# States summed on GpSimd, swapped stationaries, one transpose per four heads, and a rotary swap by DMA

## The reference, cut to what matters

```python
z = rmsnorm(h) @ w_in                       # q, kc, vc, ksl, vsl, kw, vw, gates, u
q, kc, ksl, kw = rope(...)                  # [x1*cos - x2*sin, x1*sin + x2*cos] by half heads of 32
kcmp = gelu((blocks(kc) + pe_k) @ wk1) @ wk2   # blocks of 32 tokens, stride 16: 31 of them, 2 groups
vcmp = gelu((blocks(vc) + pe_v) @ wv1) @ wv2
o = g0*softmax(q kcmp) vcmp + g1*softmax(q ksl) vsl + g2*softmax(q kw) vw
# S5: complex state per channel, x[t] = a*x[t-1] + bu[t];  y = Re(C x) + d*u;  gelu, GLU
h = h + concat(o, o_s5) @ w_out
```

## Time and profile before

| | us |
|---|---|
| median of 3 runs | 2008.1 (2006.92 to 2008.7) |
| the profiled execution: its time | 2005.77 |
| its span | 2004.0 |
| PE busy in the span | 1936.8 (97%) |
| POOL busy in the span | 336.2 (17%) |
| mean granted clock of TensorE | 0.985 |

### The profile page before, as it was taken

The page is one execution under the profiler, slowest core; times in us unless marked ns, Lnnn a source line. Parts: engine busy times, 40 slices in busy tenths (PEclk is TensorE's granted clock), DMA queues, the critical chain, the costliest instruction groups (busy, mean ns, idle before and its releaser), DMA issues.

```text
span 2004.0 us, 22537 instructions
## 1 busy us (share of the span) xinstructions
PE 1936.8 (97%) x9022; PEld 1509.8 (75%) x9022; DVE 1185.7 (59%) x1519; ACT 820.9 (41%) x1210; POOL 336.2 (17%) x329
## 2 busy tenths in 40 slices
PE   7999999999998999999999899999999899999997
PEld 5788888777644788888888778776788778776786
DVE  5748344576764556656655787826753659446732
ACT  5332233311555343213333448545542466445531
POOL 2000000135320110101011212504201024115002
PEclk9999999999998999999999899999999899999998
DMA  5232223222002145645632222221223222221331
GB/s 196 93 106 94 93 96 116 78 74 97 27 1 69 55 151 195 221 141 185 215 111 80 77 93 85 87 95 40 74 95 95 85 82 84 89 80 32 95 98 60
DMA packets 53464, 197.27 MB, mean 98 GB/s; under 512 B 6000, under 2 KB 6512, under 8 KB 52848
## 3 DMA queue, kind: packets, MB, share of 16 engines
q1 hardware_dynamic: 43200, 160.55, 24.4%
q0 software_dynamic: 7648, 29.10, 4.6%
q10 hardware_dynamic: 2512, 6.18, 0.9%
HBM read 192.67 MB, written 2.10 MB: 97 GB/s over the span
## 4 chain that ended last, share of the span: by engine, by line
PE 78%; DVE 13%; ACT 4%; issue 2%; POOL 2%; DMA 1%; ACTq 0%; POOLq 0%; DVEq 0%
PE PS L593 77%; DVE AR L1644 3%; DVE WLO L1641 2%; DVE AR L2170 1%; ACT WHI L1179 1%; DVE AR L1674 1%; DVE TMP L2244 1%; DVE AR L1995 1%; PE PS L843 1%; DVE AR L2137 0%; DMA H<-in_xT 0%; POOL ACC L2302 0%; DVE H L2073 0%; POOL AR L2339 0%; ACT SQ L1194 0%
## 5 line engine op out<-in xcount | busy, mean ns | idle before, releaser
L593 PE MATMUL PS<-HNH,WHI 128*128 128x512 f32 x1632 | 659.3, 404 | 16.4 <-ACT HNH L1210 14.6
L1641 DVE TENSOR_TENSOR WLO<-RAW,WHI 128x1024 fp32r<-128x1024 f32 (+1 forms) x272 | 374.9, 1381 | 506.7 <-ACT WHI L1179 506.6
L593 PE MATMUL PS<-HNH,WLO 128*128 128x512 f32 x1632 | 641.8, 393 | 5.9 <-DVE WLO L1641 5.9
L1179 ACT ACTIVATE WHI<-RAW 128x1024 fp32r<-128x1024 f32 (+1 forms) x272 | 297.7, 1095 | 642.2 <-PE PS L593 583.1
L593 PE MATMUL PS<-HNL,WHI 128*128 128x512 f32 x1632 | 436.3, 391 | 0.1
L593 PEld LDWEIGHTS PS<-HNH,WHI 128*128 128x128 f32 x1632 | 309.1, 189 | 96.3 <-issue 22.1
L593 PEld LDWEIGHTS PS<-HNH,WLO 128*128 128x128 f32 x1632 | 309.5, 190 | 80.4 <-issue 9.1
L593 PEld LDWEIGHTS PS<-HNL,WHI 128*128 128x128 f32 x1632 | 307.6, 188 | 64.8 <-DVE HNL L1644 1.0
L2302 POOL TENSOR_TENSOR ACC<-ACC,SQ 128x512 f32<-128x512 f32 x46 | 62.4, 1356 | 809.8 <-ACT SQ L1194 808.8
L593 PE MATMUL PS<-AR 32*128 32x256 f32 (+14 forms) x844 | 162.3, 414 | 4.4 <-POOL AR L2339 1.7
L593 PE MATMUL PS<-HIDH,WLO 128*128 128x512 f32 x352 | 137.1, 390 | 0.0
(11 more groups left out here) (314 smaller groups left out, 2295.4 us busy)
## 6 DMA issues: line engine op xcount, KB each, us to landing
RAW<-in_w_in SPq DMA_DIRECT2D x80, 512.0 KB, 3.5
AR<-in_w_ada POOLq DMA_DIRECT2D x48, 512.0 KB, 4.1
RAW<-in_w13a SPq DMA_DIRECT2D x44, 512.0 KB, 3.4
RAW<-in_w13b SPq DMA_DIRECT2D x44, 512.0 KB, 3.6
RAW<-in_w_out SPq DMA_DIRECT2D x40, 512.0 KB, 3.5
RAW<-in_w2a SPq DMA_DIRECT2D x16, 704.0 KB, 4.0
RAW<-in_w2b SPq DMA_DIRECT2D x16, 704.0 KB, 5.1
RAW<-in_w_inA SPq DMA_DIRECT2D x12, 512.0 KB, 3.4
```

What stands on the lines that cost most here:

```text
L593: return pe.matmul(o, l, r, start=start, stop=stop, skip_group_check=True)
L1179: act.activation(hi_of(name, i), raw_of(name, i), ACT.Copy).then_inc(*HI.up(name, i))
L1641: dve.tensor_tensor(lo_of(name, i), raw_of(name, i), f32(hi_of(name, i)), S_).then_inc(*LO.up(name, i))
```

## The change

Four edits, all in the mixer.

1. **States summed on GpSimd.** After `back_v` of the second tile, POOL adds the products in `SQ` into `V_`, in two operations of 128 x 512 elements. `read` then needs eight matmuls of the 16, and waits for these two sums.
2. **Compression's positions stationary.** `squeeze` moves the weights (128 columns) past the positions (62 columns stationary), with the two halves of the hidden layer on different output partitions of one bank. The hidden layer comes out turned over, so a step `hidden` transposes it back by two transposes, with two copies on ACT. The step `compressed 1` moves one item later, and writes the compressed values to four groups of partitions (eight small matmuls instead of four, four copies instead of one).
3. **Four heads per transpose.** Four transposes of 128 columns of `CE` serve two head pairs, at i = 0 and i = 2, with one copy on ACT each.
4. **The swap by DMA.** A step `swap` on ACT's queue issues four DMAs of 32 partitions each, from `TMP` to a buffer `TURNED` in SBUF; DVE's `turn` waits for them. PE has no turn any more.

Two `TURNED` buffers lie where `VT` comes later, so ACT's eviction of `v` waits for turn 7. `out_s5` passes over bank 7 where it would be next.

```diff
@@ mix_order @@
+        if i and i != 2:
+            yield "swap", i - 1          # after qk/rope i, before turn
...
+            if (z, tt) == (0, 0):
+                yield "swap", 7
...
+            if (z, tt) == (0, 1):
+                yield "hidden", 0
...
         if n == 4:
+            yield "hidden", 1
+        if n == 5:
             yield "compressed", 1
@@ pe_program @@
-                    for z in range(4):
+                    for z, (name, wr, wl) in enumerate((("state_re", CpR, CaR), ("state_im", CpI, CaI))):
+                        pe.wait_ge(*G.at(name, b))
                         for now in (True, False):
                             for j in range(2):
...
-                elif step == "turn":
-                    ps, b = take(pe, "turn", i)
-                    pe.wait_ge(*V.at("rope", i))
-                    mm(ps[:, :], ROT, TMP[:, i % 4, :], True, True).then_inc(*P_.up("turn", i))
...
-                            t = mm(hc_banks[z][mt][0][:, 0:62], w[:, i, P * mt:P * mt + P],
-                                   XBp[:, ii, :, :].rearrange("p g c -> p (g c)"), ii == 0, ii == 15)
+                            t = mm(hc_banks[z][0][64 * mt:64 * mt + 62, 0:P], XBp[:, ii, :, :].rearrange("p g c -> p (g c)"),
+                                   w[:, i, P * mt:P * mt + P], ii == 0, ii == 15)
...
+                elif step == "hidden":
+                    for mt in range(2):
+                        pe.wait_ge(*A.at("hidt", z, mt))
+                        pe.transpose(ps[:, 0:62], HIDt[r, :], IDENT[r, r]).then_inc(*P_.up("hidden", z, mt))
...
-                    if part == 0 and kind == 2:
-                        for hf in range(2):
-                                t = pe.transpose(ps[0:31, P * qt:P * qt + P], CE[:, qt, 2 * i + hf, 0:31], IDENT)
+                    if part == 0 and kind == 2 and i % 2 == 0:
+                            t = pe.transpose(ps[:, P * qt:P * qt + P], CET[i // 2][:, qt, :], IDENT)
@@ act_program @@
+                elif step == "swap":
+                    act.wait_ge(*V.at("rope", i))
+                    if n > 1:
+                        act.wait_ge(*V.at("turn", TURNS[n - 2]))
+                    for r in range(4):
+                        act.dma_start(TURNED[n % 2][32 * r:32 * r + 32, :],
+                                      TMP[32 * (r ^ 1):32 * (r ^ 1) + 32, i % 4, :]).then_inc(*loaded(f"turned{n % 2}").up(i))
...
+                        act.wait_ge(*V.at("turn", 7))      # before VT is written
@@ dve_program @@
-                    dve.wait_ge(*P_.at("turn", i))
+                    dve.wait_ge(*loaded(f"turned{n % 2}").at(i))
                     dve.wait_ge(*G.at("rope", i))
-                    dve.tensor_tensor(TMP[:, i % 4, :], bank("turn", i)[:, :], SIN, M_).then_inc(*V.up("turn", i))
+                    dve.tensor_tensor(TMP[:, i % 4, :], TURNED[n % 2], SIN, M_).then_inc(*V.up("turn", i))
@@ pool_program, back b, tile j @@
                     pool.tensor_tensor(f4(v), f4(v), c4, M_).then_inc(*G.up("back_v", t16))
+                    if j:
+                        v, turned = V_[b % 2], SQ[:, :, :]
+                        mine()
+                        for z, name in enumerate(("state_re", "state_im")):
+                            x = v[:, :, HT * z:HT * z + HT]
+                            pool.tensor_tensor(x, x, turned[:, :, HT - HT * z:T - HT * z], A_).then_inc(*G.up(name, b))
```

More of the change, by code:

```diff
@@ L389, in program @@
             loaded(f"x{k}")
-        for name in ("vecs", "consts", "s5_bc", "small_w", "pairs", "pT", "c", "rg_w", "w_if"):
+        for name in ("vecs", "consts", "s5_bc", "small_w", "pairs", "pT", "c", "rg_w", "w_if", "turned0", "turned1"):
             loaded(name)
@@ L480, in program @@
         CEa = CEf.rearrange("p (a c) -> p a c", c=32)[:, :, 0:31]
+        CET = [CEf.rearrange("p (q a c) -> p q a c", q=4, a=2)[:, :, a, :] for a in range(2)]
         Q = ar(13312, 4, T)
@@ L490, in program @@
         NEG_MAX = ar(19008, 2, 2)
+        TURNED = [ar(17408 + T * i, T) for i in range(2)]
         SUMS, SHARE = (ar(20648 + 16 * i, 2, 8).rearrange("p a (q f) -> p a q f", f=2) for i in range(2))
@@ L760, in pe_program @@
                     if c == 0:
-                        hc_banks[z] = [take(pe, "squeeze", z, mt) for mt in range(2)]
+                        hc_banks[z] = take(pe, "squeeze", z)
                     name = ("wk1", "wv1")[z]
@@ L785, in pe_program @@
                             for mt in range(2):
-                                t = mm(ps[0:31, 64 * g:64 * g + 64], HIDc[:, mt, 31 * g:31 * g + 31], WV2[:, mt, :], mt == 0, mt == 1)
+                                for a in range(2):
+                                    r = 32 * g + 64 * a
+                                    t = mm(ps[r:r + 31, 64 * g:64 * g + 64], HIDc[:, mt, 31 * g:31 * g + 31], WV2[:, mt, :], mt == 0, mt == 1)
                     t.then_inc(*P_.up("compressed", z))
@@ L1310, in act_program @@
                         act.wait_ge(*P_.at(("wk1", "wv1")[z], 3))
-                        if z:
-                            act.wait_ge(*P_.at("compressed", 0))
-                        act.activation(HIDc[:, mt, 0:62], bank("squeeze", z, mt)[:, 0:62], ACT.Gelu_apprx_tanh).then_inc(*A.up("hidc", z, mt))
+                        r = slice(64 * mt, 64 * mt + 62)
+                        act.activation(HIDt[r, :], bank("squeeze", z)[r, 0:P], ACT.Gelu_apprx_tanh).then_inc(*A.up("hidt", z, mt))
+                elif step == "hidden":
+                    z, = at_
+                    for mt in range(2):
+                        act.wait_ge(*P_.at("hidden", z, mt))
+                        act.activation(HIDc[:, mt, 0:62], bank("hidden", z, mt)[:, 0:62], ACT.Copy).then_inc(*A.up("hidc", z, mt))
                 elif step == "compressed":
@@ L1319, in act_program @@
                     else:
-                        act.activation(VC[0:31, :], bank("compressed", 1)[0:31, 0:128], ACT.Copy).then_inc(*A.up("compressed", 1))
+                        for g in range(2):
+                            for a in range(2):
+                                r = slice(32 * g + 64 * a, 32 * g + 64 * a + 31)
+                                act.activation(VC[r, 64 * g:64 * g + 64], bank("compressed", 1)[r, 64 * g:64 * g + 64], ACT.Copy).then_inc(*A.up("compressed", 1))
                 elif step == "v":
@@ L1359, in act_program @@
                         act.activation(SHARES[kind - 1], bank("shares", i, kind)[:, :], ACT.Copy).then_inc(*A.up("shares", i, kind))
[L1360 to L1364, removed]
+                        if kind == 2 and i % 2 == 0:
+                            act.wait_ge(*P_.at("ptc", i // 2))
+                            act.activation(PTC[i // 2], bank("ptc", i // 2)[:, :], ACT.Copy).then_inc(*A.up("ptc", i // 2))
                     elif i == 3 and kind == 2:
```

64 lines of the change are left out of this document (30 added, 34 removed).

## The result

| | us | ratio to before (95%) |
|---|---|---|
| before, 6 runs | 2008.05 (2003.72 to 2008.7) | |
| after, 6 runs | 2024.12 (2020.78 to 2033.75) | 1.0089 (1.0065 to 1.0112) |
| forecast | 2016 (1997 to 2025) | |

The profiled execution of after took 2033.75 (span 2032.0, mean granted clock 0.969 against 0.985).

The account below looks back on a forecast made before the run. Two chains were taken to bound the mixer, PE's own work and the one through DVE and POOL, which the sums lengthen. Terms summed to +8.6 us on 2005.77, so 2014.4, or 2016.7 as the runs' median; forecast 2016, range 1997 to 2025.

Parts of the forecast that it names:

- the term of reads 5 to 7: Attention's closed loop: read 5 costs 0.9 through DVE's scans, reads 6 and 7 end 2.1 later each; +5.1 us.
- sums in rounds 0 to 4: Front reads: POOL's sums delay PE and DVE's scans, 0.9 + 2.2 + 2.2, with 4.0 for the clock.
- squeezes, hidden, compressed: -1.7 in round 1 with turn 4; in attention three squeezes save 2.6, hidden and compressed take back 0.6: -2.0.
- four heads: Attention: fewer transposes of CE give 3.0 us, of which 0.5 falls before a wait: -2.5.
- what bounds the kernel: Mixer: PE's own work and the chain through DVE and POOL run side by side, with hardly a microsecond between them.
- sign of being wrong: Front half: wrong if squeeze 0,2 ends earlier than at 470.8, or read 3 before 509.
- the clock after reads 0 and 1: New PE idles of 5 and 4 us lower the granted clock: 2.0 us each, bounds 0 and 2.8, in all +4.0.
- the other six swaps: ACT's queue: 2.5 us each, priced at nothing; up to 2 each if DVE's turn came before the landing.
- squeeze 0,0 and 0,2: Up to their ends PE is bound by its own work; a turn and a squeeze save 0.85 + 0.86: -1.7 each.
- The swap of turn 0: Round 0: the DMA lands at 432.0, so DVE, and POOL behind it, are 2.1 us late.
- that only the sums cost: Rival: turns, squeezes and transposes gain 15.1 us, the sums lose 5, giving 1998; chance 0.17.
- That PE's work is the bound: Rival: PE's work is the bound after all, so all 22.5 us go, giving 1986; chance 0.10.

Follow-up runs that it names:

- the kernel with PE kept busy: The kernel before with the sums alone, plus overwritten 128x128 matmuls that keep PE busy ahead of reads: 2019.44 us, 1.0066.
- The kernel with the squeezes: The kernel before with the squeezes' operands swapped and four heads per transpose, no sums and no swap: 2006.74 us, 1.0004.
- the two kernels of after's kind with a landing of 2.1: One is after with added overwritten matmuls keeping PE busy at reads, 2027.01 us; the study does not say outright which the other is.
- the other kernel: The kernel before with the sums alone, plus overwritten 128x128 matmuls ahead of reads: 2019.44 us, 1.0066; the 64x64 matmuls were added to after, 2027.01 us.

## Why the prediction was right in direction and half as large as it came

The step that failed is the term of reads 5 to 7, priced at +5.1 without a change of the clock: it measured +11.6. The sum of +8.6 can be split by the kernels above, with 17.9 measured:

| term | forecast | measured |
|---|---|---|
| sums in rounds 0 to 4 (0.9 + 2.2 + 2.2, clock 4.0) | +9.3 | +10.0 (7.2 to 12.6) |
| sums in rounds 5 to 7 | +5.1 | +11.6 (9.0 to 14.0) |
| swap by DMA with the turns removed (+2.1 - 1.7) | +0.4 | +4.8 (2.6 to 7.0) |
| squeezes, hidden, compressed (-1.7 - 2.0) | -3.7 | +2.2 (about -1 to +5.4), or +6.0 with the bank's wait |
| four heads | -2.5 | -5.2 (-7.6 to -3.0) |
| the last three together | -5.8 | +0.4 (-2.0 to +2.8) |

The parts don't add up exactly. The two rows of the sums and the last one make 22.0, which agrees with 17.9 within the intervals; the three rows of single edits make far more than the +0.4 of the three together, as they were measured in other surroundings.

- **Right: what bounds the kernel.** The sums stand between POOL's last product and PE, POOL's 17% notwithstanding. PE waits at all eight reads, 6.2 us at read 0, 4.3 at read 1, 8 at read 2 and least at reads 3 and 4, and squeeze 0,0 to read 3 is a chain over weight load, DVE and POOL. Neither sign of being wrong came: squeeze 0,2 ends at 480 and read 3 at 521. But PE's busy time, which was to fall by 15 to 20 us, rose by 1.0, as the rest ran slower.
- **Failed: reads 5 to 7**, +5.1 measured as +11.6. I counted two delays of 2.1 and one of 0.9 and put the clock at none. The loop was closed as I said, but each read also leaves PE idle for 3.4 to 5.0 us, and then the scores and transposes on which DVE and ACT wait run at the lower level (1.09 became 1.97). In the profile of the kernel with the sums in rounds 5 to 7, read 5 to read 6 took 2.0 us more than before, read 6 to read 7 4.3 (9.7 became 14.1), and the same stretch behind read 7 4.2. Behind read 6 the same instructions, from the transposes to the values, took 4.7 us for 3.0; behind read 7 the kernel with PE kept busy, at a clock of 1.00, was 2.0 faster (14.4 for 16.4). So the 2.1 each were right, and about as much again is the clock. Read 5's 2.0 for 0.9 is not: with the clock at 1.00 this stretch took the same 21.2 us, and why stays open. I had the row on the clock, and used it at reads 0 and 1 alone.
- **Mis-sized: the clock after reads 0 and 1**, 2.0 each with a bound of 2.8. It was 3.2 and 2.6 with the sums alone, and 3.9 after read 0 in after. The earlier trace rows has one window, and in after three of them in a row, from 436 to 460, are at 0.79, 0.50 and 0.86. That the front half as a whole held (+10.0 for +9.3) is in part luck: something else in it cost less than I said, and no run shows what.
- **Wrong: "edits at nothing, the other six swaps".** I asked whether ACT's queue was free and not what else was on the way. Swap 3 is issued with the weight loads, and PE, made faster, moves it nearer to them. The bound that I gave, 2 us each if DVE came before the landing, was the right kind of answer; 6.1 was its size. In the profile of after itself turn 3 doesn't wait, since squeeze 0,0 comes late and holds the loads back.
- **Mis-sized: squeeze 0,0 and 0,2, -1.7 each,** and three more in attention. The kernel with the squeezes has squeeze 0,0 1.8 us earlier, as I said (448.3 against 450.1), and 0,2 at 467.4 against 469.0; by read 3 it is 1.3 later than before. A saving ahead of the load that starts the chain was to be a gain, and what took it was a wait for a bank, which nothing in my account looked at.
- **Mis-sized in the other direction: four heads,** 5.2 for 2.5. The interval begins at 3.0, the work itself; what is above that isn't settled (in its profile the clock is 1.00 from 604 to 620, where before had 0.87 and 0.91, but 0.59 from 636 to 644, where before had 0.79).
- **The swap of turn 0** was to be 2.1 late. It was 3.6 late in after and without the sums (landing 4.2), and 1.1 to 1.3 in the swap alone and in the two kernels of after's kind with a landing of 2.1; 2.1 lies between. What it costs by itself is open, as said.

The rivals: that only the sums cost (1998) named the right edit and gave the rest a gain that isn't there. That PE's work is the bound (1986) is excluded by the time, that the clock stays up by the windows.

The Trainium skill's page "SBUF — State Buffer", section "Terms", says that the port pair shared by DVE and GpSimd is an exclusive lock, held for a whole instruction. The rows around read 0 show that form: the carry (L1930), 0.17 before, takes 1.05 beside a sum of 1.26, and the next (L1932), 0.16 before, takes 1.19. With sums a quarter as wide, 0.44 each, they take 0.24 and 0.38, and without sums 0.17 and 0.16. Here a small instruction of DVE took up to nearly as long as the POOL operation that it met.

## What to carry to other kernels

Moving work from the engine with 97% to the one with 17% cost time here, because the new place lies between that engine's last product and its consumer; ask first what is behind the consumer in its queue. A wait of several us on TensorE is to be priced with the matmuls that follow it at 1.2 GHz, wherever someone waits for those, in every round and not at the first ones alone. And an edit that frees time on PE moves transfers too: look for which DMA it will meet, and which bank comes up.

## What was not expected of the hardware

- A swap by four DMAs of 64 KB each within SBUF: one landed 2.1 us after issue in the median, 4.2 when a load of 512 KB was issued 0.1 us behind it (2.1 when 0.3 or more lay between) and 5.4 beside two such loads. Issuing the four took 2.4 to 3.7 us of ACT's queue.
- TensorE's busy time rose by 1.0 us with some 22.5 us of work removed: at 1.2 GHz the records are longer.
- The clock was 0.50 in a window in which PE was busy for all 8 us, after a wait of 1.53 and with 64 x 64 matmuls, and 1.00 with 128 x 128 ones in the other kernel. Why is open: the two kernels differ in more than that.
